# RWKV chunk inverses on 32x32 diagonal tiles up to level 16, one off-diagonal block at level 32, and a solve in two parts

## The reference, cut to what matters

```python
lhs = jnp.eye(RW_CHUNK, dtype=f32) - L_ab          # L_ab strictly lower triangular, 64x64 for each chunk and head
W1 = lax.linalg.triangular_solve(lhs, a_dec, left_side=True, lower=True, unit_diagonal=True)
U0 = lax.linalg.triangular_solve(lhs, jnp.einsum('bnhts,bnhsv->bnhtv', L_ak, v),
                                 left_side=True, lower=True, unit_diagonal=True)
```

## Time and profile before

| | |
|---|---|
| median of 3 runs | 3167.13 us |
| the profiled execution | 3168.01 us, its span 3166.1 us, 1.9 us outside it |
| TensorE busy | 3031.2 us (96% of the span) |
| TensorE weight loads busy | 2495.2 us (79%) |
| GpSimd busy | 2332.5 us (74%) |
| VectorE busy | 1405.2 us (44%) |
| ScalarE busy | 634.1 us (20%) |
| mean granted TensorE clock | 0.987 of full |
| the four RWKV cores of layer 0 | 689.8 to about 904 us of the span |
| the four RWKV cores of layer 1 | 2261 to about 2476 us |

### The profile page before, as it was taken

The page is one execution under the profiler, slowest core; times in us unless marked ns, Lnnn a source line. Parts: engine busy times, 40 slices in busy tenths (PEclk is TensorE's granted clock), DMA queues, the critical chain, the costliest instruction groups (busy, mean ns, idle before and its releaser), DMA issues. The chain is left out here.

```text
span 3166.1 us, 46915 instructions
## 1 busy us (share of the span) xinstructions
PE 3031.2 (96%) x19746; PEld 2495.2 (79%) x19746; DVE 1405.2 (44%) x1839; ACT 634.1 (20%) x1031; POOL 2332.5 (74%) x1877
## 2 busy tenths in 40 slices
PE   8999999889999999999899999998899999999996
PEld 7888877777778888888778888777777788888884
DVE  4221233766646563211852214248666475622127
ACT  1000125443310020000310002453433100200011
POOL 8988786533249989888899888865331599899875
PEclk9999999999999999999999999999999999999998
DMA  4332332111113333322233323311210133333322
GB/s 141 100 100 94 100 120 61 43 50 39 29 41 94 126 95 105 100 94 100 87 95 105 95 98 107 107 55 36 55 36 27 54 94 126 100 107 94 100 87 87
DMA packets 202029, 267.86 MB, mean 85 GB/s; under 512 B 12352, under 2 KB 130460, under 8 KB 201692
## 3 DMA queue, kind: packets, MB, share of 16 engines
q1 hardware_dynamic: 195200, 244.82, 25.4%
q10 hardware_dynamic: 6620, 20.04, 1.8%
HBM read 258.52 MB, written 6.29 MB: 84 GB/s over the span
## 5 line engine op out<-in xcount | busy, mean ns | idle before, releaser
L1148 POOL TENSOR_TENSOR w_hi<-w_raw,zero 128x512 fp32r<-128x512 f32 (+2 forms) x936 | 1075.4, 1149 | 726.9 <-PE ps L846 685.4
L1151 POOL TENSOR_TENSOR w_lo<-w_raw,w_hi 128x512 fp32r<-128x512 f32 (+2 forms) x936 | 1283.7, 1371 | 73.2
L846 PE MATMUL ps<-hT_hi,w_hi 128*128 128x512 f32 (+1 forms) x2368 | 930.2, 393 | 16.9 <-POOL w_lo L1151 11.8
L846 PE MATMUL ps<-hT_hi,w_lo 128*128 128x512 f32 (+1 forms) x2368 | 906.5, 383 | 0.0
L846 PE MATMUL ps<-hT_lo,w_hi 128*128 128x512 f32 (+1 forms) x2368 | 906.5, 383 | 0.0
L846 PEld LDWEIGHTS ps<-hT_hi,w_hi 128*128 128x128 f32 x2368 | 444.6, 188 | 122.5 <-POOL w_lo L1151 22.7
L846 PEld LDWEIGHTS ps<-hT_hi,w_lo 128*128 128x128 f32 x2368 | 444.3, 188 | 89.2
L846 PEld LDWEIGHTS ps<-hT_lo,w_hi 128*128 128x128 f32 x2368 | 445.0, 188 | 84.3 <-issue 2.9
L1711 DVE TENSOR_TENSOR act_raw<-silu,ps 128x512 f32<-128x512 f32 x88 | 59.9, 681 | 620.6 <-PE ps L846 620.6
L846 PE MATMUL ps<-w_hi,aT_hi 128*128 128x512 f32 x704 | 274.6, 390 | 0.0
L846 PE MATMUL ps<-w_lo,aT_hi 128*128 128x512 f32 x704 | 274.0, 389 | 0.0
(11 more groups left out here) (305 smaller groups left out, 3663.0 us busy)
## 6 DMA issues: line engine op xcount, KB each, us to landing
w_raw<-in_w_in SPq DMA_DIRECT2D x104, 512.0 KB, 3.6
w_raw<-in_ffn_wg SPq DMA_DIRECT2D x176, 256.0 KB, 2.8
w_raw<-in_ffn_wu SPq DMA_DIRECT2D x176, 256.0 KB, 3.1
w_raw<-in_ffn_wd SPq DMA_DIRECT2D x88, 512.0 KB, 3.6
w_raw<-in_w_in SPq DMA_DIRECT2D x96, 128.0 KB, 2.3
w_raw<-in_w_out SPq DMA_DIRECT2D x16, 512.0 KB, 3.7
w_raw<-in_ple_gate SPq DMA_DIRECT2D x16, 512.0 KB, 3.7
ln_rows<-in_ln_g ACTq DMA_DIRECT2D x8, 512.0 KB, 4.2
```

What stands on the lines that cost most here:

```text
L846: ins = nc.tensor.matmul(o, l_, r_, start=first, stop=last, skip_group_check=into is not None)
L1148: nc.gpsimd.tensor_tensor(w_split[0][:, q, kk, 0:w], w_raw[:, r, kk, 0:w], zero[:, 0:1].to_broadcast([P, w]), ALU.add).then_inc(*step("w_h ...
L1151: nc.gpsimd.tensor_tensor(w_split[1][:, q, kk, 0:w], w_raw[:, r, kk, 0:w], w_split[0][:, q, kk, 0:w].bitcast(F32), ALU.subtract).then_inc( ...
```

## The change

The inverse of each 64x64 matrix is now built as two inverses of its 32x32 diagonal blocks, four tiles `g` per unit pair of chunks (`quad(g)` is partitions 32g to 32g + 31), and one off-diagonal block of 32x32.

- A product over all diagonal tiles (`quads`) is 8 units x 4 = 32 matmuls of 32x32 with 32 columns, on the four diagonal 32x32 tiles of the array.
- `first_quads` makes both the transposed tiles and the tiles themselves by products with the identity: 64 matmuls. VectorE now makes `invT` from the bank too, so after `rwx_done`, and before `inv`.
- Levels 1 to 4 keep their form, with 32 matmuls a block in place of 16. VectorE's operands have half the columns.
- Level 5: `last_strips` and `last_widen` are 16 matmuls each, on two tiles off the diagonal. VectorE's work there is two copies of 32 partitions each in place of a memset and a masked product, and two such copies in place of the sum of L731.
- The solve is in two parts that add up in the same PSUM banks. `solve_diagonal` (32 matmuls, 128 columns) stands right behind `last_strips`, ahead of level 5's fill. `solve_rest` (16 matmuls, 128 columns) stands where the solve stood.

```diff
+            def quads(b, left, right):
+                for hd, t in UNITS:
+                    for g in range(4):
+                        ins = nc.tensor.matmul(b[quad(g), quad_cols(hd, t)], left(hd, t, g), right(hd, t, g), start=True, stop=True)
+                return ins
...
+            def first_quads():
+                b = take(("rwx", L, ft, 0), ("rw_inv", L, ft, 0))
...
+                        nc.tensor.matmul(b[quad(g), c], quad_of_pairs(hd, t, g, g), eye, start=True, stop=True)
+                        ins = nc.tensor.matmul(b[quad(g), 256 + c.start:256 + c.stop], eye, quad_of_pairs(hd, t, g, g),
+                                               start=True, stop=True)
...
             def strips(lev):
...
+                quads(b, lambda hd, t, g: quad_of_pairs(hd, t, g, g), diagonal(inv)).then_inc(*step("rwx_done", L, ft, lev))
             def widen(lev):
...
+                quads(b, diagonal(invT), diagonal(xl)).then_inc(*step("rwi_done", L, ft, lev))
...
+                quads(b, diagonal(xl), diagonal(invT)).then_inc(*step("rwj_done", L, ft, lev))
...
+            def solve_diagonal():
+                pe.wait_ge(*after("rw_lakv", L, ft))
+                pe.wait_ge(*after("rw_tok", L, ft, 1))
+                pe.wait_ge(*after("rw_invT", L, ft, top - 1))
...
+                    for t in range(NT):
+                        for g in range(4):
+                            ins = nc.tensor.matmul(b[quad(g), t * P:(t + 1) * P], invT[quad(g), NT * hd + t, 0:QUAD],
+                                                   rhs[quad(g), hd, t, :], start=t == 0, stop=False, skip_group_check=True)
...
+            def solve_rest():
+                pe.wait_ge(*after("rw_invT", L, ft, top))
...
+                            ins = nc.tensor.matmul(b[quad(late), t * P:(t + 1) * P], invT[quad(early), NT * hd + t, QUAD:HEAD],
+                                                   rhs[quad(early), hd, t, :], start=False, stop=t == NT - 1, skip_group_check=True)
...
+                if lev == top:
+                    last_strips()
+                    solve_diagonal()
                 advance(fill[lev])
-                widen(lev)
+                if lev < top:
+                    widen(lev)
+                else:
+                    last_widen()
...
             advance(fill["last"])
...
+            solve_rest()
             advance(fill["solve"])
...
             def keep_strips(lev):
+                now("rwx_done", L, ft, lev)
+                got = bank_quads(bank("rwx", L, ft, lev))
+                if lev == top:
+                    for cp in range(2):
+                        late = quad(2 * cp + 1)
+                        ins = v.tensor_copy(xl[late, :, 0:QUAD], got[late, :, :])
+                    ins.then_inc(*step("rw_x", L, ft, lev))
+                    return
...
-            v.tensor_tensor(invT[:, :, :], bm[:, :, :, 0, :].rearrange("p d t n -> p (d t) n"), all_units(mask64(R64_INVT)),
-                            ALU.mult).then_inc(*step("rw_invT", L, ft, 0))
             now("rwx_done", L, ft, 0)
-            v.tensor_tensor(inv[:, :, :], bank_units(bank("rwx", L, ft, 0)), all_units(mask64(R64_INV)), ALU.mult).then_inc(
+            v.tensor_tensor(invT[:, :, 0:QUAD], bank_quads(bank("rwx", L, ft, 0), 1), all_units(mask32(B_INVT)), ALU.mult).then_inc(
+                *step("rw_invT", L, ft, 0))
+            v.tensor_tensor(inv[:, :, 0:QUAD], bank_quads(bank("rwx", L, ft, 0)), all_units(mask32(B_INV)), ALU.mult).then_inc(
                 *step("rw_inv", L, ft, 0))
```

More of the change, by code:

```diff
@@ L85, in constants @@
     blocks += [r < n, r <= n]
[L86 to L87 removed]
+    r2, n2 = i % QUAD, np.arange(QUAD)[None, :]
+    blocks += [r == n, pair(r2, n2, 1) | (r2 == n2), pair(n2, r2, 1) | (r2 == n2)]
+    blocks += [pair(r2, n2, h) for h in RX_LEVELS[1:-1]]
     blocks += [pair(j, i, h) for h in HG_LEVELS]
@@ L409, in widen @@
                 pe.wait_ge(*after("rw_invT", L, ft, lev - 1))
[L410 to L416, removed]
+                b = take(("rwi", L, ft, lev), ("rw_inv", L, ft, lev))
@@ L422, in widen, with last_widen @@
-                ins.then_inc(*step("rwj_done", L, ft, lev))
+                        early, late = 2 * cp, 2 * cp + 1
+                        ins = nc.tensor.matmul(b[quad(late), quad_cols(hd, t)], quad_of_pairs(hd, t, early, late),
+                                               inv[quad(early), NT * hd + t, 0:QUAD], start=True, stop=True)
+                ins.then_inc(*step("rwx_done", L, ft, top))
+            def last_widen():
+                pe.wait_ge(*after("rw_x", L, ft, top))
+                b = take(("rwj", L, ft, top), ("rw_invT", L, ft, top))
+                for hd, t in UNITS:
+                    for cp in range(2):
+                        early, late = 2 * cp, 2 * cp + 1
+                        ins = nc.tensor.matmul(b[quad(early), quad_cols(hd, t)], xl[quad(late), NT * hd + t, 0:QUAD],
+                                               invT[quad(late), NT * hd + t, 0:QUAD], start=True, stop=True)
+                ins.then_inc(*step("rwj_done", L, ft, top))
@@ L429, in rwkv_core_pe @@
             advance(fill["pairs"])
-            strips(0)
+            first_quads()
             pairs(1, k_inv)
@@ L724, in core_dve @@
                     now("rw_inv", L, ft, lev - 1)
-                    early = of_units(inv[:, :, :], hgt, 0)
-                    v.tensor_tensor(early, early, of_units(bank_units(bank("rwi", L, ft, lev)), hgt, 0), ALU.add).then_inc(
+                    early = of_units(inv[:, :, 0:QUAD], hgt, 0)
+                    v.tensor_tensor(early, early, of_units(bank_quads(bank("rwi", L, ft, lev)), hgt, 0), ALU.add).then_inc(
                         *step("rw_inv", L, ft, lev))
                 now("rwj_done", L, ft, lev)
[L729 to L732, removed]
+                got = bank_quads(bank("rwj", L, ft, lev))
+                if lev < top:
+                    now("rw_invT", L, ft, lev - 1)
+                    late = of_units(invT[:, :, 0:QUAD], hgt, 1)
+                    v.tensor_tensor(late, late, of_units(got, hgt, 1), ALU.add).then_inc(*step("rw_invT", L, ft, lev))
+                else:
+                    for cp in range(2):
+                        early = quad(2 * cp)
+                        ins = v.tensor_copy(invT[early, :, QUAD:HEAD], got[early, :, :])
+                    ins.then_inc(*step("rw_invT", L, ft, lev))
                 aside(2)
```

81 lines of the change are left out of this document (51 added, 30 removed).

## The result

| | before | after |
|---|---|---|
| median | 3166.71 us (4 runs, 3165.64 to 3170.24) | 3232.01 us (4 runs, 3230.55 to 3233.15) |
| ratio | 1 | 1.0205 (95% interval 1.0192 to 1.0217) |
| profiled execution | 3168.01 us | 3231.28 us, span 3229.5 us |
| mean granted clock | 0.987 | 0.972 |

The kernel got 65 us slower. The forecast was 3147 us with a range up to 3191. So it is outside the range and on the wrong side.

A forecast was written before the change was run, and what follows sets the result against it. TensorE, busy 96% of the span, was taken as the bound. Net gains of 2.8, 1.8, 3.15 and 2.5 us for a layer's cores gave 20.5 us over two layers, so 3147 us, range 3130 to 3191.

The forecast's parts named there:

- the serial rival: TensorE issues a record every 28.5 ns whatever the tiles: 15.7 us lost a core, 3290 us; chance 0.05.
- the forecast's 3.8 us a core: TensorE's gain without new waits: blocks save 5.8 us, the solve costs 1.7 and shape changes 0.3.
- A record of 32x32 at 8 ns: Blocks on four tiles: 31 ns in a tile for 32 columns, so 8 ns a record, 0.51 us a block.
- The weak point that the prediction named: For four-tile blocks, no profile row showed 64 records in a row at 8 ns.
- The six starts of rows 5: Six records at the turn from L515 to L501, read as 12 ns apart; evidence on how fast TensorE can issue.
- The rival "32 columns cost what 64 do": Each tile takes 57 ns a record, 14.3 ns over four: 2.9 us lost a core, 3189 us; chance 0.18.
- `last_widen` 0.5 us: Level 5's two blocks of 32 records on two tiles, 15.5 ns a record, 0.99 us together.
- `solve_diagonal` and `solve_rest` 1.7 us each: The two-part solve takes 1.70 and 1.74 us a core, 1.70 more than the solve before.
- New waits for `inv` and the gated output, 1 to 2 us a core: TensorE's uncovered waits for VectorE: 0.2 us at each of four levels and at level 0, more in core 1.
- The 1.0 us that core 1 was to wait: VectorE's side steps in core 1 deliver `inv` at 6.1 us where TensorE wants it at about 5.1.
- VectorE sets the pace: Rival: long VectorE side steps make cores 0 to 2 wait 0.8 us more at two levels each, 3157 us; chance 0.13.
- The clock rival: TensorE falls to 1.2 GHz within the cores, some 10 us a core; one such core gives about 3158 us; chance 0.04.

The follow-up runs named there:

- x1_streams: Separate kernel without the reference's computation: five streams of matmuls of different tile shapes; 32x32 with 32 columns on four tiles averaged 27.4 ns a record.
- x2_double: The kernel before, with each matmul of the inverse's strips and widen issued twice; 3274.98 us in one run.
- x3_spread: The changed kernel with the same instructions, fill groups of levels 2 to 4 spread around and between widen's two blocks; 3230.9 us, ratio 1.0201.
- x4_single: The changed kernel with the solve in one part again, 16 matmuls of 64x64; 3220.97 us, ratio 1.0167.
- x5_dup: The changed kernel with the update of `invT` issued twice at levels 1 to 4; 3301.08 us, ratio 1.0422.
- x7_top: The kernel before with only level 5 cut to 32x32 off-diagonal blocks, instruction count unchanged; 3164.4 us, ratio 0.9991.
- x6_pauses: Separate kernel without the reference's computation: whole-array bursts with pauses of three lengths, then a 32x32 stream of 96 columns; that stream took 20.9 us.

## Why the prediction was wrong

**The step that failed** is the end of the serial rival: "A shortfall of instructions would look alike: 157 pages took 0.3% of 16 engines, about 1 us a page of 256 instructions, and a level will want some 400 in 4 us. This fits if pages are fetched ahead." With it the sum put the supply of instructions at nothing. They are not fetched far enough ahead. The 1 us is the time in which a page's packets move; from its start to the first record it is 2.39 us (after, median), and in x1_streams the next page started 1.0 to 1.6 us after the burst before it, which makes 3.45 to 4.0 us for 256 instructions. With that price in place of 1 us the same sentence gives 400 instructions x 13.5 ns = 5.4 us for a level of 4 us. As an estimate, with every core's level like this one of core 1, 1.4 us too much at four levels of eight cores is 45 us, near the 50.9 us of the 28 stops. The question was asked, but the price was not looked for. The kernel before bounds it from one side alone: its own 64x64 blocks, at 28.5 ns a record, ran without a stop of this kind.

**Where the 65.9 us in the cores come from**, by the tally of both layers (distances over 0.9 us between starts of TensorE's records, waits for VectorE included, and time at 1.2 GHz, both for the profiled execution):

| | cores of layer 0, us | layer 1 | stops, us, both layers | at 1.2 GHz, us |
|---|---|---|---|---|
| before | 222.4 | 221.8 | 14.7 | 15.7 |
| after | 247.7 | 262.4 | 66.3 | 115.6 |
| x2_double | 275.5 | 275.7 | 10.9 | 16.2 |
| x3_spread | 250.5 | 255.5 | 71.3 | 80.8 |
| x4_single | 246.3 | 252.8 | 74.3 | 110.8 |
| x5_dup | 290.5 | 281.3 | 109.6 | 138.9 |
| x7_top | 220.6 | 221.0 | 17.9 | 15.6 |

The stops grew by 51.6 us. The array's gain is worked out: the forecast's 3.8 us a core, less some 0.8 for 8.9 ns a record in place of 8 (896 x 0.9 ns), 24 us in eight cores. The remainder, 65.9 - 51.6 + 24 = 38 us, is left for the 99.9 us more at 1.2 GHz, which can take half of that at most, 50, and for stops shorter than 0.9 us. The traces of before and after give an estimate of the share. I set each distance at 1.2 GHz, outside the stops, against the mean distance of the same pair of lines and shapes at full clock: the excess is 6 us before and 41 after, so some 35 us go with the low clock, short stops inside that time included. The five distances of L348 belong to it too, which leaves 46.6 us for the growth of the stops; 65.9 - 46.6 - 35 + 24 leaves 8 us for short stops at full clock and for what this does not tell apart.

**The steps one by one.**
- A record of 32x32 at 8 ns: 8.9 in L391. Right, a little low. The weak point that the prediction named, 64 records in a row, was none; more than a page in a row was. The six starts of rows 5 were read as 12 ns apart; in the trace they come in groups, four within 9 ns (731.743 to 731.752), so they spoke less for the rivals than the prediction allowed.
- The rival "32 columns cost what 64 do": wrong, 8.9 and not 14.3 ns. 8.9 ns on four tiles is 36 ns in each, where 64 columns took 57. The Trainium skill's rule (TensorEngine Tiling (Array Packing), section Instruction Overhead) does not describe these blocks; by it the time would have been 3189 us, nearer to the result than my forecast, but for a reason that the trace refutes.
- `last_widen` 0.5 us, `solve_diagonal` and `solve_rest` 1.7 us each: right (x4_single: 11 us for the split in place of 13.6).
- New waits for `inv` and the gated output, 1 to 2 us a core: the chain was right and the wait was over-sized. The list of waits does not show it, since a record's 0.18 us covers it. But from the start of `widen(1)` at 700.01 to the first record of the strips at 701.24 it is 1.23 us, forecast 1.24, and in 21 of the 32 levels the strips start 0.15 us after VectorE's `inv`. The two blocks in front take 1.14 us and not 1.02, so what is left of the wait is 0.1 us in place of 0.2. The 1.0 us that core 1 was to wait before the strips of level 5 came to 0.1 us between starts in layer 0 and 0.6 in layer 1. Whether VectorE would be later without the stops, which give it time, stays open.
- VectorE sets the pace: no. Its sums took 0.29 us, as forecast.
- The serial rival, 3290: a block is not serial, but over a dense page the mean is near what that rival said of a record, 27 ns and more where it had 28.5. The kernel loses less than its 15.7 us a core, 8.2. Some 95 pages start in the cores after and 28 stops stand there; that the fills, 0.23 us a record, give the other pages time to arrive is the reading that fits.
- The clock rival: it happened, 0.85 to 0.94 in layer 0's cores, and it came with the stops; that the stops alone cause it is not shown. Its "some 10 us a core" would give 8 x 10 x 99.9/510 = 16 us for the 99.9 us more at the low level, of 510 in the cores; the estimate above is 35, since the rival counted the fills alone.

**What stays open.** What the 2.4 us between a page's start and its first record are made of, of which its packets fill about 1; and how many instructions are at hand when a page is ordered. At after's 28 stops, 0 to 246 records and weight loads, 60 in the median, started between the page's start and the stop. And whether the clock would have stayed up with shorter stops, or falls with small tiles by themselves.

## What to carry to other kernels

Count instructions for each microsecond as a resource of its own. On this chip a stream of TensorE got 256 instructions in 3.45 to 4.0 us, 27 to 31 ns for a matmul record with its weight load: work that is denser than that over more than a page stood still, and work of 28.5 ns a record did not. Cutting a product into smaller tiles cost 65 us where it raised the count in dense stretches, and did no harm where it left the count alone (x7_top). In a profile, the sign is a stop in the middle of a block, with "issue" as its releaser and a 16 KB transfer on the instruction queue that starts 2.2 to 2.8 us before its end. Take out the waits for other engines before you count: a page stands ahead of some of them by chance.

## What the runs showed of the hardware that was not expected

- Four 32x32 tiles take a record every 8.9 ns, with 32 columns, at full clock, as long as instructions are at hand.
- The delay from the start of an instruction page to TensorE's next record was 2.39, 2.46 and 2.39 us in the median, in after, x3_spread and x5_dup, three kernels with different work around the stops.
- A stream with the whole array busy without a stop, 32 columns at a time, had a granted clock of 0.50 (x1_streams, 216.4 to 314 us), and so had the stream of 32x32 tiles with 32 columns, in bursts with 1.5 to 2.2 us idle; the one with 64 columns and 1.47 us idle had 1.00. Idle times of 2.0 us between bursts of 1.3 us led to 0.58, of 1.15 us to 1.00 (x6_pauses).
